# Differential attention and convolution placed between the quarter pieces of an in-projection, and the opening loads reordered

## The reference, cut to what matters

```python
proj = hn @ w_in                      # 256 x 3072: xc, b_gate, c_gate, q, k, v of 512 columns each
u = c_gate * xc
y = b_gate * (u * w[2] + shift(u, 1) * w[1] + shift(u, 2) * w[0])      # shifts go along the tokens
y_conv = rms_norm over 8 groups of 64 columns (y) * conv_out_g
q, k = rms_norm over 64 columns (q, k), times q_norm_g / 8, k_norm_g    # 4 heads x 2 halves x 64
p = softmax(causal(q @ k.T))          # for each of 4 heads and of its 2 halves
a = p[half 0] - lam * p[half 1];  out = a @ v                           # v: 128 columns per head
y_attn = rms_norm over 128 columns (out) * subln_g * (1 - lam_init)
h = h + concat(y_conv, y_attn) @ w_out                                  # 1024 x 1024
# then: rms_norm, routing to 2 of 32 experts, and the experts' weights (192 MB) streamed from HBM
```

## Time and profile before

| | us |
|---|---|
| median of 3 runs | 1704.05 (1702.71 to 1706.43) |
| the profiled execution: time, span | 1702.44, 1700.7 |
| PE busy | 1474.1 (87%) |
| DVE busy | 759.4 (45%) |
| ACT busy | 611.5 (36%) |
| POOL busy | 44.0 (3%) |
| mean granted clock of TensorE | 0.935 |

### The profile page before, as it was taken

How to read it: one execution, slowest core, us unless ns; L and a number is a source line. 1 busy time by engine, 2 the same in 40 slices (tenths; PEclk the granted TensorE clock), 3 DMA queues, 4 the chain that set the end, 5 groups by cost and what they waited for, 6 DMA issues and landing times.

```text
span 1700.7 us, 22405 instructions
## 1 busy us (share of the span) xinstructions
PE 1474.1 (87%) x8731; PEld 1130.4 (66%) x8731; DVE 759.4 (45%) x986; ACT 611.5 (36%) x773; POOL 44.0 (3%) x70
## 2 busy tenths in 40 slices
PE   5999999599999999999999999967687767766766
PEld 4888887588888888877788887855554434424433
DVE  3545547845455545465454546675521120221121
ACT  4434445344344534367454345433210110111010
POOL 4000000000000000000010000040000000000000
PEclk9999989899999999999999999977799888989888
DMA  6565544135555564553365544531599999999997
GB/s 208 188 207 173 191 155 156 43 99 191 204 176 189 169 208 172 206 169 122 124 203 174 204 166 172 199 112 69 228 403 418 418 417 417 418 419 418 418 417 303
DMA packets 170748, 397.13 MB, mean 234 GB/s; under 512 B 9329, under 2 KB 107713, under 8 KB 154321
## 3 DMA queue, kind: packets, MB, share of 16 engines
q1 hardware_dynamic: 169152, 392.20, 62.0%
q0 software_dynamic: 1424, 4.32, 0.9%
q10 hardware_dynamic: 128, 0.03, 0.0%
HBM read 394.94 MB, written 1.58 MB: 233 GB/s over the span
## 4 chain that ended last, share of the span: by engine, by line
PE 70%; DMA 11%; SPq 9%; DVE 6%; ACT 3%; issue 1%; ACTq 0%; DVEq 0%
PE psum L245 20%; PE psum L247 19%; PE psum L246 19%; DMA pair_ring<-in_w_exp_up 9%; SPq L1776 8%; PE psum L1821 4%; PE psum L1842 2%; PE psum L1861 1%; DMA pair_ring<-in_w_exp_down 1%; PE psum L524 1%; DVE low L240 1%; ACT high L236 1%; ACT hT_high L399 1%; PE psum L1147 1%; DVE scratch L1061 0%
## 5 line engine op out<-in xcount | busy, mean ns | idle before, releaser
L240 DVE TENSOR_TENSOR low<-raw,high 128x2048 fp32r<-128x2048 f32 x180 | 408.7, 2290 | 147.4 <-ACT high L236 144.7
L245 PE MATMUL psum<-high,hT_high 128*128 128x512 f32 x1088 | 437.9, 402 | 20.7 <-DVE low L240 13.9
L247 PE MATMUL psum<-high,hT_low 128*128 128x512 f32 x1088 | 429.1, 394 | 0.0
L246 PE MATMUL psum<-low,hT_high 128*128 128x512 f32 x1088 | 428.5, 394 | 0.0
L236 ACT ACTIVATE high<-raw 128x2048 fp32r<-128x2048 f32 x180 | 340.3, 1912 | 82.6 <-PE psum L247 79.5
L245 PEld LDWEIGHTS psum<-high,hT_high 128*128 128x128 f32 x1088 | 207.6, 191 | 65.9 <-issue 15.5
L247 PEld LDWEIGHTS psum<-high,hT_low 128*128 128x128 f32 x1088 | 207.2, 190 | 45.1
L246 PEld LDWEIGHTS psum<-low,hT_high 128*128 128x128 f32 x1088 | 207.8, 191 | 41.1
L1842 PE MATMUL psum<-pair_ring,scratch 128*32 128x256 f32 x2048 | 140.6, 424 | 57.4 <-DMA pair_ring<-in_w_exp_up 56.1
L1842 PEld LDWEIGHTS psum<-pair_ring,scratch 128*32 128x32 f32 x2048 | 67.0, 119 | 129.1 <-DMA pair_ring<-in_w_exp_up 77.9
L665 DVE TENSOR_TENSOR aT_low<-psum,aT_high 128x512 fp32r<-128x512 f32 x40 | 27.7, 692 | 252.1 <-ACT aT_high L627 252.1
(11 more groups left out here) (305 smaller groups left out, 1193.1 us busy)
## 6 DMA issues: line engine op xcount, KB each, us to landing
pair_ring<-in_w_exp_gate SPq DMA_DIRECT2D x64, 1024.0 KB, 22.1
pair_ring<-in_w_exp_up SPq DMA_DIRECT2D x64, 1024.0 KB, 22.8
pair_ring<-in_w_exp_down SPq DMA_DIRECT2D x64, 1024.0 KB, 22.4
raw<-in_ffn_w_gate SPq DMA_DIRECT2D x88, 512.0 KB, 4.1
raw<-in_ffn_w_up SPq DMA_DIRECT2D x88, 512.0 KB, 5.3
raw<-in_ffn_w_down SPq DMA_DIRECT2D x88, 512.0 KB, 4.0
raw<-in_gla_w_in SPq DMA_DIRECT2D x24, 512.0 KB, 4.6
raw<-in_sb_w_in SPq DMA_DIRECT2D x24, 512.0 KB, 4.5
```

What stands on the lines that cost most here:

```text
L240: dve.tensor_tensor(low[:, p % RING, :], raw_of(p), high[:, p % RING, :].bitcast(F32), ALU.subtract).then_inc(split, 1)
L245: pe.matmul(psum_out, lhs_high, rhs_high, start=start, stop=False, skip_group_check=True)
L246: pe.matmul(psum_out, lhs_high, rhs_low, start=False, stop=False, skip_group_check=True)
L247: return pe.matmul(psum_out, lhs_low, rhs_high, start=False, stop=stop, skip_group_check=True)
```

## The change

The in-projection of the mixing stage takes the quarter form that the stick-breaking stage has (now `in_quarters`, called by both): three PSUM banks in turn, and after each quarter (12 matmuls) a hook, `after(n, r)`. From it PE turns q and k, forms the scores and turns the weights. DVE and ACT get written-out orders in which pieces, norms, scores and softmaxes alternate; ACT now makes both tiles' copies. The mask is added in PSUM, and the exponentials are read from there. The gains of q and k are applied by ACT when it copies the turned rows. The convolution goes from POOL to DVE, and u is shifted by four DMAs inside SBUF instead of through HBM. The products with v come behind the in-projection; the out-projection begins on the convolution's columns and turns the attention's columns after three half pieces.

In the opening the first layer's gains are loaded, turned and copied alone; the other 48 rows follow after the first products. Piece 0 is rounded and split in halves, piece 1 before tile 1 of x. POOL's small loads wait until two pieces are rounded, and those of the two row gains until the end of the first layer.

```diff
         def mix_pe(pe):
...
-            in_pe(pe, "mix_in", 7, between)
...
+            def after(n, r):
+                at = 4 * n + r
+                if at == 6:
+                    turn_qk(0)
+                elif at == 10:
+                    turn_qk(1)
+                elif at == 12:
+                    dots(0)
+                elif at == 13:
+                    dots(1)
+                elif at == 15:
+                    turn_a(0)
+                    dots(2)
+                elif at == 16:
+                    turn_a(1)
+                    dots(3)
+                elif at == 19:
+                    turn_a(2)
+                elif at == 20:
+                    turn_a(3)
...
+            in_quarters(pe, "mix_in", 7, after)
+
+            def front(products):
+                pe.wait_ge(h_ready, H_AT["mix"] + 1)
+                for tt in range(TT):
+                    turn_half(tt, 0)
+                outs()
+                pe.wait_ge(turn_low, 4 * MIX_TURN + 1)
+                products(0, 0)
+                pe.wait_ge(turn_low, 4 * MIX_TURN + 2)
+                products(0, 1)
+                products(1, 0)
+                for tt in range(TT):
+                    pe.wait_ge(h_ready, H_AT["mix"] + 2 + tt)
+                    turn_half(tt, 1)
+                products(1, 1)
+                pe.wait_ge(turn_low, 4 * MIX_TURN + 4)
+            out_pe(pe, "mix_out", 8, front)
...
+        def mix_dve(dve, step):
...
+            def conv():
+                acc = both(CG, D_CONV)
+                dve.tensor_tensor(acc, both(XC, D_CONV), weight(2), ALU.mult)
+                dve.wait_ge(m["shifted"], 4 * 16)
+                dve.wait_ge(m["cleared"], 1)
+                dve.tensor_tensor(by_tile(shifted[0]), by_tile(shifted[0]), weight(1), ALU.mult)
+                step(dve.tensor_tensor(by_tile(shifted[1]), by_tile(shifted[1]), weight(0), ALU.mult))
+                step(dve.tensor_tensor(acc, acc, by_tile(shifted[0]), ALU.add))
+                step(dve.tensor_tensor(acc, acc, by_tile(shifted[1]), ALU.add))
...
+                dve.tensor_tensor(acc, acc, both(BG, D_CONV), ALU.mult).then_inc(m["conv"], 1)
...
+            piece(8)
             dve.wait_ge(m["lam_exp"], 1)
...
             scores(0)
             scores(1)
+            weights(0)
+            piece(9)
+            weights(1)
...
+            scores(2)
+            dve.tensor_tensor(both(XC, D_CONV), both(XC, D_CONV), both(CG, D_CONV), ALU.mult).then_inc(m["u"], 1)
+            piece(10)
+            scores(3)
+            weights(2)
+            weights(3)
+            piece(11)
+            piece(12)
+            dve.wait_ge(m["u"], 1)
+            conv()
+            piece(13)
+            conv_norm()
...
         def mix_conv_pool(pool, step):
+
             pool.wait_ge(m["u"], 1)
...
             for i in range(2):
-                pool.dma_start(by_tile(shifted[i]), conv_rows[1 - i:1 - i + TOKENS, :].rearrange("(a p) n -> p a n", p=P)
...
+                n = i + 1
+                pool.dma_start(by_tile(shifted[i])[n:P, :, :], both(XC, D_CONV)[0:P - n, :, :]).then_inc(m["shifted"], 16)
+            for i in range(2):
+                n = i + 1
+                pool.dma_start(shifted[i][0:n, D_CONV:2 * D_CONV], proj[P - n:P, 0, XC:XC + D_CONV]).then_inc(m["shifted"], 16)
...
-            act.wait_ge(gainT_set, 1)
             x_turn_act(act, 0, 0)
-            round_piece(act, 0)
+            act.wait_ge(*landed_of(0, 0))
+            first_half = slice(0, SLOT // 2)
+            act.activation(high[:, 0, first_half], raw[:, 0, first_half], ACT.Copy).then_inc(first_rounded, 1)
+            act.activation(high[:, 0, SLOT // 2:], raw[:, 0, SLOT // 2:], ACT.Copy).then_inc(rounded, 1)
+            round_piece(act, 1)
             x_turn_act(act, 0, 1)
-            round_piece(act, 1)
...
             x_turn_dve(dve, 0, 0)
-            split_piece(dve, 0)
...
+            split_piece(dve, 1)
             x_turn_dve(dve, 0, 1)
-            split_piece(dve, 1)
```

More of the change, by code:

```diff
@@ L731, in in_pe, with in_quarters, quarter @@
                         products(n, half, tt)
+        def in_quarters(pe, name, k_norm, after):
+            b, done = FIRST_PIECE[name], IN_CHUNKS * IN_ORDER.index(name)
+            def quarter(n, half, tt):
+                q, at = b + 2 * n + half, 2 * n + tt
+                pe.wait_ge(split, q + 1)
+                if half == 0 and at >= 3:
+                    pe.wait_ge(in_copied[(at - 3) % 2], done + (at - 3) // 2 + 1)
+                for k in range(4):
+                    kk, tok = 4 * half + k, slice(tt * P, (tt + 1) * P)
+                    ins = product(pe, banks(at % 3), hT_high[:, kk, tok], hT_low[:, kk, tok], four_k(high, q)[:, k, :],
+                                  four_k(low, q)[:, k, :], start=kk == 0, stop=kk == KD - 1)
+                if tt == 1:
+                    ins.then_inc(used, 1)
+                elif half == 1:
+                    ins.then_inc(in_first, 1)
+            first_products(pe, k_norm, lambda half, tt: quarter(0, half, tt))
+            for n in range(1, IN_CHUNKS):
+                for r in range(4):
+                    quarter(n, r // 2, r % 2)
+                    after(n, r)
         def in_act(act, name, k_norm, between=lambda n: None):
@@ L776, in products @@
                     ins.then_inc(used, 1)
[L778 to L792, removed]
+            front(products)
             products(2, 0)
@@ L1097, in sb_pe @@
         def sb_pe(pe):
[L1098 to L1112, removed]
+            done = IN_CHUNKS * IN_ORDER.index("sb_in")
             def turn_q(n):
@@ L1181, in after, with front @@
                     outs(0)
[L1183 to L1187, removed]
+            in_quarters(pe, "sb_in", 4, after)
             for j in range(1, OUT_PIECES):
                 outs(j)
-            out_pe(pe, "sb_out", SB_TURN, None, 5, by_piece=True)
+            def front(products):
+                for j in range(2):
+                    pe.wait_ge(turn_low, 4 * SB_TURN + j + 1)
+                    for tt in range(TT):
+                        products(j, tt)
+                pe.wait_ge(turn_low, 4 * SB_TURN + 4)
+            out_pe(pe, "sb_out", 5, front)
         def sb_act(act, step):
@@ L1332, in dots, with turn_a @@
[L1332 to L1336, removed]
+                for c in range(2):
+                    rows, dst = slice(DA_HD * c, DA_HD * (c + 1)), banks(dot_banks(hd) + c)
+                    ins = pe.matmul(dst[:, P:HEAD], mqT[rows, at + P:at + TOKENS], mkT[rows, at:at + TOKENS],
+                                    start=False, stop=True, skip_group_check=True)
+                    ins.then_inc(m["dots"], 1)
+            def turn_a(hd):
@@ L1396, in mix_act @@
-            act.wait_ge(m["out"], 1)
+            copies(3)
+            piece(10)
+            turned_a(0)
+            softmax(2)
+            turned_a(1)
+            softmax(3)
+            piece(11)
+            copies(4)
+            piece(12)
+            turned_a(2)
+            turned_a(3)
+            piece(13)
+            conv_root_act()
+            copies(5)
+            act.wait_ge(used, b + IN_PIECES)
             for tt in range(TT):
-                act.activation(square[:, tt * D_CONV:(tt + 1) * D_CONV], banks(6 + tt), ACT.Square).then_inc(m["sq"], 1)
-                act.wait_ge(m["sum"], tt + 2)
-                act.activation(stat[:, 48 + 4 * tt:52 + 4 * tt], stat[:, 16 + 4 * tt:20 + 4 * tt], ACT.Sqrt,
-                               scale=1.0 / DA_V, bias=eps[:, :]).then_inc(m["root"], 1)
+                high_half(tt, 0, tt + 1)
@@ L1402, in mix_act @@
             for tt in range(TT):
-                turn_act(act, MIX_TURN, tt)
+                act.wait_ge(m["out"], tt + 1)
+                act.activation(square[:, tt * D_CONV:(tt + 1) * D_CONV], banks(ATTN_BANK[tt]), ACT.Square).then_inc(m["sq"], 1)
+                act.wait_ge(m["sum"], tt + 4)
+                act.activation(out_stat(tt, "root"), out_stat(tt, "sum"), ACT.Sqrt, scale=1.0 / DA_V,
+                               bias=eps[:, :]).then_inc(m["root"], 1)
+            piece(14)
+            for tt in range(TT):
+                high_half(tt, 1, tt + 3)
```

445 lines of the change are left out of this document (260 added, 185 removed).

## The result

The changed kernel takes **1688.35 us** (median of 4 runs, 1687.0 to 1692.22), the kernel before, run beside it, 1704.41; the ratio is 0.9912, with a 95% interval of 0.9898 to 0.9925. Forecast were 1668 us, with a range from 1657 to 1682. So the change makes the kernel faster by 16 us, 20 less than the forecast 36, and outside the range. The profiled execution has a span of 1685.5.

A forecast was written before the change was run, and what follows sets the result against it. PE's idling in the mixing stage, whose end sets the experts' weight stream, and in the opening was taken as the bound; 9.4 (opening) + 26.8 (mixing stage) = 36.2 off 1704.05 gives 1667.9, forecast 1668 us, range 1657 to 1682.

The forecast's parts named there:

- are 8 behind u: Mixing stage: shifted rows land at 1119.7, DVE needs them at 1126.5; up to 6.8 more, or twice the landing time, free.
- the rival of a longer DVE queue: Mixing stage: tiny operations are DVE's own or PSUM operands and waits cost more; 1685, or 1676 with half; chance 0.18.
- Opening: Kernel start: first product at 11.6, 6.0 wait gone, piece 2 at 28.0 instead of 37.5; gain 9.4 us.
- The in-projection's end: Mixing stage: attention work of 6.3 us and a 1.2 wait added inside; end at 1132.0, 1122.6 on the new clock.
- DVE's queue: Mixing stage: splits, scores, weights, convolution and norm from 1095.5 sum to 43.9 us; the convolution's columns ready at 1139.4.
- the stall 7.4: End of the in-projection: PE waits from 1132.0 for the convolution's columns, a new stall of 7.4 us.
- the short price: Mixing stage: tiny DVE operations take 0.2 to 0.3 us without POOL's tensor work; long ones would add 17 us.
- Behind it: Convolution turning and products with v 4.4, out-projection 23.7, slow start 2.7; sum 30.8 us, stage ending at 1170.2.
- the slower case: Rival: the clock stays low through both projections, some 380 matmuls at 0.43 instead of 0.23; 1744 us; chance 0.03.
- that of no effect: Rival: the experts' weight stream starts no earlier, so the change does nothing; 1704 us; chance 0.02.
- the prediction's own signs: Wrong if in-projection split waits exceed 3 us, its end wait is under 3 or over 12, or expert-load and stage-end shifts differ.
- a smaller gain of another kind, between 1685 and 1700: Whole kernel: a leftover case in the list of chances, given 0.04.

The follow-up runs named there:

- experiment 8: experiment 7's kernel with ACT taking x's two square sums in its opening waits around piece 1's rounding; 1658.80 us (0.973).
- experiment 1: the changed kernel with only the 127-partition shifting DMA issued as two, of 112 and 15 partitions; 1667.79 us (0.9787).
- experiment 10: the kernel before with only the mixing stage's part of the change, the 127-row shift split into 112 and 15; 1676.41 us (0.9834).
- experiment 7: experiment 1's kernel with v's products before turning the convolution's columns, DVE's convolution before piece 12's split, piece 13's split behind the norm; 1662.77 us (0.9748).
- experiment 5: the kernel before with only the reordered opening; 1697.29 us (0.9958).

## Why the prediction missed

**The step that failed** is one sentence of the mixing stage: four issues in a row and 5.8 to landing "are 8 behind u", with 6.8 to spare and twice the landing time as the upper bound. They landed at 1140.2, 36.7 behind u's end at 1103.5. The price came from the nearest row by size, 512 KB, but that was a load of 128 partitions; the new transfer has 127, and the row says nothing on that. The issues were too cheap as well: the first two took 4.46 us. The sentence even had the rule for the loss, "beyond that each us costs one": DVE waited 21.95, PE's hole grew from 6.8 to 28.8, and splitting the transfer gave 20.6 in time. So the mechanism stood and the size of one term did not. What failed with it is the range. Its upper end came from the rival of a longer DVE queue, and this transfer, the one thing with no row of its own shape, had been bounded at twice its neighbour. A worse bound was to be had from the profile: one engine of the 16 that move 412 GB/s when full moves 26, and 508 KB at 26 take 20 us. But it would not have sufficed. With 2.2 us of issues ahead, the rows land 22.2 behind u, 7.4 too late for DVE, and that gives 1675, still in the range. What the bound lacks is in the trace: of the copy's 127 packets of 4 KB 100 start behind 1117, 49 of them in the 14 us to 1131, where the engine is shared with the weight loads. At 0.16 each they would have taken 8, so I estimate the sharing at 6 to 7 us, and the start, some 8 behind u instead of 2.2, at the other 6.

**Opening** (forecast 9.4, measured 8.2 in the profile, 7.9 in time). First product 11.47 for 11.6; piece 1 landed by 12.73 for 13; piece 2's products 27.58 for 28.0. What was missing is the clock: behind the idle 1.85 the matmuls ran at 1.2 GHz from 28.5 on (0.43 from one to the next instead of 0.23) for some nine of them, 1.6 to 1.8 us. I had kept that price for waits of some 6 us; in experiment 8 PE waits 0.17 there and the clock stays up.

**The in-projection's end**: 1122.6 forecast, 1124.0 measured. Its first product, moved by the opening alone, was forecast at 1058.7 - 9.4 = 1049.3, and PE's timeline has it at

```profile
1051.57 0.76 PE L243 MATMUL psum<-high,hT_high 128*128 128x512 f32 x1 [0.32 <-DVE low L238]
```

so only 7.1 of the opening's 8.2 had come through to it, and where the 1.1 went is open. The stretch itself took 72.4 instead of 73.3: PE has no wait inside, and the 1.2 that were allowed for one were not needed.

**DVE's queue**: the columns were forecast for 1139.4 - 9.4 = 1130.0 and came at 1131.6 in experiment 1, so 1.6 late, about what the opening gave less (with its measured 8.2 it would be 1131.2); the stall 7.4, and 6.8 there. The tiny operations took 0.23, the short price, so the reading of the earlier trace rows holds for a stage without tensor work on POOL.

**Behind it**: 30.8 forecast from the columns to the stage's end. Experiment 1, around the end of the wait, with the slow start inside:

```profile
1128.00:1132.00 4.00, 0.40 (x2) 0.40 (x3) 3.10 (x4) 1.46 (x3) 0.00 (x0) 0.59 0.00 0
1132.00:1136.00 4.00, 4.00 (x23) 4.00 (x22) 1.44 (x3) 1.79 (x3) 0.00 (x0) 0.56 0.00 0
1136.00:1140.00 4.00, 4.00 (x25) 3.52 (x24) 3.20 (x10) 1.93 (x4) 0.00 (x0) 1.00 0.02 4
```

The slow clock is there for some 4 us from 1131.6 on, near the forecast 5. For the stage's end 1170.2 - 9.4 = 1160.8 were forecast. SP's loads for experts in experiment 1 come at

```profile
1160.88 0.34 SPq L1946 DMA_DIRECT2D pair_ring<-in_w_exp_gate  x1
...
1197.57 0.37 SPq L1946 DMA_DIRECT2D pair_ring<-in_w_exp_gate  x1
```

against 1196.92 and 1232.76, 36.0 and 35.2 earlier. The first is issued when the last weight piece has been used, so the end is right to a tenth. That is luck in part: the columns came 1.6 late, and the stretch behind them took 29.3 instead of 30.8. What made it shorter no run separates. In time the stage gives 26.7 (experiment 10), where the forecast was 26.8.

**The rivals**: but for the slow start of each, the clock was at 1.00 in both projections, so the slower case did not come; the gain reached the end, so that of no effect did not either. Two of the prediction's own signs tell that it is wrong: PE's wait at the in-projection's end is over 12, and the shifted copies landed behind DVE's need. The 0.04 for "a smaller gain of another kind, between 1685 and 1700" was where the truth lay, and it had no mechanism. With the shift in time the sum comes out, with misses of 1 to 2 us that cancel; one term of 22 us was missing, and it alone took the time out of the range.

## What to carry to other kernels

Before a transfer is priced by its bytes, look at how many partitions it has: a copy shifted by one row has 127, went through one DMA engine at 26 GB/s here, slower still beside other loads, and the loss can be had back for one more issue (112 + 15). The sign in a profile is a DMA share of 0.06 that lasts; which transfer it is, a shared semaphore doesn't tell, a split of one at a time does. And the operation of a change whose like is in no row, however small its part in the sum, wants a bound by what the machine could do at worst, shared with what else runs then, and not by twice its neighbour.

## What the runs showed of the hardware

- A DMA of 127 or 113 partitions from SBUF to SBUF ran on one engine of 16, at 25 to 27 GB/s, from POOL's queue (both counts) and from ACT's (127). While weight loads were under way, half of that engine's packets were theirs: 20 and 20 from 1124 to 1130.
- From POOL's queue such a DMA came with many more packets, 2272 against 384 for the same rows in 112 + 15. It was not the data that was cut small: in both kernels they lie in 253 packets of 4 KB, and 1904 of the others are packets of 8 bytes, 15 KB in all. What these are for, the trace doesn't say. The two issues took 4.46 us instead of 2.05 for three. From ACT's queue there were none of them (521 packets for 1.04 MB), and the rate was the same, so they are not what made it slow.
- The issue behind such a DMA on ACT's queue took 14.48 us.
- PE's clock fell to 0.50 behind an idle of 1.85 us in the opening of the changed kernel. Behind 2.43 it fell in experiment 7 (0.61 in the mean from 28 to 32) and stayed at 1.00 in experiment 5; these are single executions, and the runs don't say what made the difference.
- Maxima taken from PSUM with the mask added in place took DVE 0.69, 0.42, 0.68 and 0.17 a head, 1.86 in its queue because they overlap a little; the prediction took 2.0 between bounds of 1.6 and 2.5.
